# Value rows of one block gathered alternately with the next block's input rows, in two places

## The chip, the cores and the metric

One Trainium2 chip, one core of it. TensorE (PE) multiplies matrices, VectorE (DVE) and ScalarE (ACT) work elementwise, GpSimd (POOL) here only issues the indirect row gathers, SyncE (SP) issues most other transfers. All transfers share the core's 16 DMA engines. The metric is device time of the whole program in microseconds, the median over runs.

## The reference, cut to what matters

One decoder layer over 512 prompt tokens and 8 sample tokens with a cache of 4096 positions each. The part around the change is the product-key expert layer, run over blocks of 128 tokens, and beside it the sample tokens' attention over the paged cache.

```python
def one_block(xb):                       # 128 tokens
    q = jnp.einsum('td,de->te', xb, w_peer_q).reshape(PEER_BLOCK, PEER_HEADS, 2, PEER_DKEY // 2)
    s = jnp.einsum('thpc,hpkc->thpk', q, peer_sub_keys, preferred_element_type=jnp.float32)
    top_s, top_i = lax.top_k(s, PEER_TOPK)
    ...
    expert = jnp.take_along_axis(cand_i, best_pos, axis=-1)
    gate = jax.nn.softmax(best_s, axis=-1)
    u = peer_u[expert]
    act = jax.nn.gelu(jnp.einsum('thkd,td->thk', u, xb, preferred_element_type=jnp.float32), approximate=False)
    return jnp.einsum('thk,thkd->td', (gate * act).astype(peer_v.dtype), peer_v[expert])
```

## The kernel before

After projections and prompt attention the expert layer runs over four blocks of 128 tokens. For each block TensorE *routes* (`route(b)`: transposes of the normed rows, four query projections, their transposes, four products with the sub-keys; ScalarE copies each result in `route_copies(b)`), and VectorE chooses 16 experts for each of 8 heads (`top_subkeys_of`, `top_experts`; semaphore `top_done`). Then two phases follow.

In the *input phase* (u) GpSimd gathers 128 times one row of `peer_u` per token (slot k of every token, 128 rows of 4 KB in one gather), and VectorE takes the dot product with the token's row (`u_dots`, L1365). At the end ScalarE applies gelu, and TensorE and VectorE lay the weights out (`turn_w`, `W_done`). In the *value phase* (v) GpSimd gathers per token k its 128 rows of `peer_v`, with the transposed index `idxT`, and TensorE multiplies them by the token's weights (`v_phase`, L1902, two halves; the second half of row k is issued after the first half of row k + 1, and with it the row is given free). Both phases use one ring of eight slots (`RING = 8`); gather number r waits until slot r - 8 is free. In the program GpSimd's order is: inputs of block 0, values of block 0, inputs of block 1, and so on; with block 3's values the sample tokens' own rows alternate, by a list (`LAST_ROWS`).

Beside it runs the sample tokens' attention over the cache, in units: SyncE loads unit n (four pages, buffers for four units, `load_unit`), TensorE forms scores and key norms (`score_step`, L1964 to L1994), ScalarE squares (`score_units`, L879), VectorE combines eight units to a chunk (`combine_chunk`, L1396). The first 17 units (`K_U1`) stand on TensorE between route(3) and block 1's values, 15 (`K_V1`) are stepped beside block 1's value rows, one unit per eight rows from row 8 on, 28 (`K_U2`) stand between block 1's and block 2's values, and four beside block 2's values. ScalarE's gelu of a block stands behind the squares of the units before it. The constants for this part are loaded by SyncE once the last routing score of block 3 is copied, and the units' loads stand behind them.

VectorE's small work inside an input phase hangs on the dot before which it stands: the dict handed to `u_phase` gives the slot k for each piece (addition of the previous block's result `add_y`, copy of the transposed index `copy_idxT`, `finish_gates`, the queries for the cache part, chunks).

TensorE's order around the change: route(1), weights of block 0, all values of block 0, route(2), index of block 1, route(3), the cache part's queries, `K_U1`, weights of block 1, values of block 1 with `K_V1`, index of block 2, `K_U2`, block 2.

## Time and profile before

| | us |
|---|---|
| median of 3 runs | 2368.76 |
| lowest and highest | 2368.74, 2373.32 |
| span of the profiled execution | 2358.0 |
| median less profiled span | 10.8 |

| engine | busy us (share) |
|---|---|
| TensorE matmul | 1745.8 (74%) |
| VectorE | 1134.5 (48%) |
| ScalarE | 355.3 (15%) |
| GpSimd | 1232.7 (52%) |
| DMA: 784.77 MB | 333 GB/s mean |

The busy shares are averages over a program whose stages differ. Stage windows, which give each engine's busy time, the share of the DMA engines that is busy and the bytes per second between two times, tell more: their columns are start:end, length, then the busy time of TensorE's matmuls, its weight loads, VectorE, ScalarE and GpSimd. The input gathers' queue and the value gathers' queue are one (GpSimd's software queue, 547.43 MB), the cache units come through SyncE's (231.08 MB).

### The profile page before, as it was taken

To read this page: it belongs to the slowest core of one execution; us is meant where nothing else is said; L and a number is where in the kernel's file an instruction comes from. 1 tells how busy PE (TensorE), PEld (TensorE's weight loads), DVE (VectorE), ACT (ScalarE), POOL (GpSimd) and SP (SyncE) were. 2 spreads that over 40 slices of the span, in tenths; PEclk is the share of its full clock that TensorE was granted. 3 is DMA by queue.
4 is the path that set the end of the run, shared out by engine and by line. 5 is a ranking of instruction groups with operands and counts; after the bars stand their busy time and mean duration, and the time that the engine had idled before them with its cause. 6 is when DMAs were issued, how large, how long until landed. Compare 5 with 4: busy or idle time off the path is not lost.

```text
span 2358.0 us, 32033 instructions
## 1 busy us (share of the span) xinstructions
PE 1745.8 (74%) x11231; PEld 710.9 (30%) x11231; DVE 1134.5 (48%) x2727; ACT 355.3 (15%) x761; POOL 1232.7 (52%) x1076
## 2 busy tenths in 40 slices
PE   8999849857777858789998888897566223337878
PEld 2555836522011433333333333331112000011212
DVE  1543888877503666645005676691000455551361
ACT  1222223301000113221112223221000000000000
POOL 0000236657767658836567886756333444564665
PEclk9999969979999879889999799999888555558999
DMA  5104548899999899999999999999999999999988
GB/s 219 27 23 181 194 148 278 293 412 330 345 369 358 307 318 399 399 323 377 399 400 366 368 399 397 398 386 366 403 401 401 408 404 404 404 384 355 349 308 316
DMA packets 258555, 784.77 MB, mean 333 GB/s; under 512 B 36593, under 2 KB 45450, under 8 KB 254938
## 3 DMA queue, kind: packets, MB, share of 16 engines
q0 software_dynamic: 150784, 547.43, 61.3%
q1 hardware_dynamic: 106442, 231.08, 26.4%
q10 hardware_dynamic: 1168, 4.23, 0.5%
q8 instruction: 88, 1.44, 0.2%
q14 instruction: 73, 0.60, 0.1%
HBM read 775.80 MB, written 6.81 MB: 332 GB/s over the span
## 4 chain that ended last, share of the span: by engine, by line
PE 40%; DMA 29%; SPq 9%; issue 7%; DVE 7%; POOL 5%; another core or an unknown queue 2%; ACT 1%; ACTq 0%; DVEq 0%; POOLq 0%
DMA arena<-peer_v,idxT 12%; DMA arena<-peer_u,eidx 10%; PE ps L1902 9%; PE ps L1964 7%; PE ps L1588 7%; POOL arena L552 5%; DMA arena<-vn_pool 4%; SPq L514 3%; DVE arena L1365 3%; SPq L511 3%; PE ps L1828 3%; DMA arena<-kpe_pool 2%; SPq L509 2%; PE ps L1950 2%; PE ps L1703 2%
## 5 line engine op out<-in xcount | busy, mean ns | idle before, releaser
L552 POOL DMA_INDIRECT arena<-peer_u,eidx x512 | 659.2, 1287 | 666.8 <-PE ps L1817 275.2
L1365 DVE CUSTOM_DVE_ANT_0 arena<-arena 128x1024 f32<-128x1024 f32 x512 | 619.6, 1224 | 697.3 <-DMA arena<-peer_u,eidx 672.8
L552 POOL DMA_INDIRECT arena<-peer_v,idxT x512 | 519.7, 1015 | 423.9 <-PE ps L1902 309.3
L1902 PE MATMUL ps<-arena 128*32 128x512 f32 x2048 | 554.5, 646 | 115.9 <-DMA arena<-peer_v,idxT 96.7
L1964 PE MATMUL ps<-arena 128*128 128x512 f32 x512 | 314.4, 700 | 45.7 <-DMA arena<-kpe_pool 43.3
L2034 PE MATMUL ps<-arena 128*32 128x512 f32 x512 | 104.6, 882 | 265.6 <-DMA arena<-vn_pool 264.1
L1902 PEld LDWEIGHTS ps<-arena 128*32 128x32 f32 x2048 | 105.1, 114 | 448.6 <-DMA arena<-peer_v,idxT 309.4
L879 ACT ACTIVATE arena<-ps 128x512 f32<-128x512 f32 x256 | 150.8, 596 | 462.1 <-PE ps L1964 273.9
L1588 PE MATMUL ps<-arena 128*128 128x512 f32 (+3 forms) x400 | 172.0, 584 | 0.4 <-DVE arena L1028 0.4
L1950 PE MATMUL ps<-arena 128*32 128x128 f32 x2048 | 148.2, 288 | 16.4 <-issue 8.7
L1964 PEld LDWEIGHTS ps<-arena 128*128 128x128 f32 x512 | 82.8, 202 | 106.6 <-issue 56.8
L1950 PEld LDWEIGHTS ps<-arena 128*32 128x32 f32 x2048 | 73.0, 111 | 123.9 <-issue 105.3
L2034 PEld LDWEIGHTS ps<-arena 128*32 128x32 f32 x512 | 13.5, 128 | 295.9 <-DMA arena<-vn_pool 146.1
L1828 PE MATMUL ps<-arena 128*128 128x512 f32 x192 | 90.5, 630 | 7.8 <-issue 5.1
L1588 PEld LDWEIGHTS ps<-arena 128*128 128x128 f32 (+1 forms) x400 | 66.7, 171 | 92.7 <-issue 92.2
L1980 PE MATMUL ps<-arena 128*32 128x128 f32 x2048 | 88.5, 289 | 5.1 <-issue 5.1
L1980 PEld LDWEIGHTS ps<-arena 128*32 128x32 f32 x2048 | 66.7, 115 | 60.1 <-issue 50.0
L901 ACT ACTIVATE arena<-ps 128x128 f32<-128x128 f32 x32 | 8.9, 278 | 458.5 <-PE ps L2012 338.1
L1703 PE MATMUL ps<-arena 128*128 128x512 f32 x128 | 62.2, 628 | 12.5 <-DVE arena L1156 12.5
L1666 PE MATMUL ps<-con,arena 128*128 128x128 f32 x160 | 28.6, 303 | 42.5 <-ACT arena L716 39.9
L1828 PEld LDWEIGHTS ps<-arena 128*128 128x128 f32 x192 | 38.1, 202 | 54.4 <-issue 51.0
L716 ACT ACTIVATE arena<-ps,nmx 128x128 f32<-128x128 f32 (+3 forms) x64 | 33.4, 527 | 132.4 <-DVE nmx L1126 117.7
(310 smaller groups left out, 1566.8 us busy)
## 6 DMA issues: line engine op xcount, KB each, us to landing
arena<-kt_pool SPq DMA_DIRECT2D x256, 320.0 KB
arena<-vn_pool SPq DMA_DIRECT2D x256, 320.0 KB
arena<-w_q SPq DMA_DIRECT2D x16, 1024.0 KB, 13.7
arena<-w_in SPq DMA_DIRECT2D x8, 1236.0 KB, 15.7
arena<-w_o SPq DMA_DIRECT2D x16, 512.0 KB, 5.1
arena<-w_q SPq DMA_DIRECT2D x4, 2048.0 KB, 11.3
arena<-peer_u,eidx POOLq DMA_INDIRECT x512
arena<-peer_v,idxT POOLq DMA_INDIRECT x512
```

What stands on the lines that cost most here:

```text
L511: sp.dma_start(kbuf[:, slot, j, :], src[bass.ds(pg, 1), :, :] .rearrange("a p n -> p (a n)")).then_inc(k_in[slot], 16)
L552: pool.indirect_dma_start(ring[:, q % RING, :], None, table, bass.IndirectOffsetOnAxis(ap=index, axis=0)).then_inc(g[q % RING], 16)
L879: nc.scalar.activation(sqd[:, m % 2, :], ps[:, 2 + m % 2, :], ACT.Square).then_inc(sqd_done, 1)
L1365: V_.tensor_tensor_reduce(rows, rows, x, 1.0, 0.0, ALU.mult, ALU.add, acc[:, k:k + 1]).then_inc(u_used, 1)
L1588: ins = T_.matmul(ps[0:n, i, 0:w], xn[t % 2][:, c, 0:n], win[:, c, 512 * i:512 * i + w], start=(c == 0), stop=(c == DC - 1))
L1703: last = T_.matmul(ps[:, OPB[b] + i, :], mixT[b][:, c, :], wo_ch[c][:, 512 * i:512 * i + 512], start=(c == 0), stop=(c == DC - 1))
L1828: last = T_.matmul(ps[:, RB[b][i], :], xT2[:, c * P:(c + 1) * P], wq[:, c, 512 * i:512 * i + 512], start=(c == 0), stop=(c == DC - 1))
L1902: return T_.matmul(ps[32 * j:32 * j + 32, i, :], W32[:, j, c, :], ring[:, q % RING, 512 * i:512 * i + 512], start=(c == 0), stop=(c == 31) ...
L1950: last = T_.matmul(ps[32 * j:32 * j + 32, 4 + s % 2, 2 * P:3 * P], dcon[:, E_HM + 32 * (4 * par + q):E_HM + 32 * (4 * par + q) + 32], sqd[ ...
L1964: T_.matmul(ps[:, 2 + m % 2, :], wkd[:, q * P:(q + 1) * P], kbuf[:, slot, :, 512:640], start=True, stop=True).then_inc(n_ps, 1)
L1980: T_.matmul(ps[32 * j:32 * j + 32, 4 + s % 2, 0:P], qz[:, c, 2 * j + par, :], kbuf[:, slot, j, c * P:(c + 1) * P], start=(par == 0 and c = ...
L2034: T_.matmul(ps[32 * j:32 * j + 32, 4 + par, :], pTd[:, s % 2, 32 * j:32 * j + 32], kbuf[:, slot, j, 0:512], start=False, stop=True, tile_p ...
```

## The change

The rows' order becomes one list for the whole program, `SEQ`: the inputs of block 0, then for each block its first `LEAD[b]` value rows, then input rows of the next block alternating with the rest of the value rows, then the rest of the inputs. `LEAD = [72, 80, 128]`: block 0's values alternate from token 72 with block 1's inputs, block 1's from token 80 with block 2's inputs, block 2's not at all. GpSimd walks the list. TensorE's routes of blocks 2 and 3 are cut into ten steps each and stand between the value rows of block 0, at tokens 70, 73, 76 and so on up to 124. VectorE's small pieces in the input phases of blocks 1 and 2 move to later slots, since those that need the end of the previous block's values can't stand before slot 56 and 48. ScalarE stores the first result after both routes' copies.

```diff
+LEAD = [72, 80, 128]
...
-        LAST_ROWS = []
+        SEQ = [("u", 0, k) for k in range(P)]
+        for b in range(NB - 1):
+            SEQ += [("v", b, k) for k in range(LEAD[b])]
+            for k in range(P):
+                SEQ.append(("u", b + 1, k))
+                if LEAD[b] + k < P:
+                    SEQ.append(("v", b, LEAD[b] + k))
...
+            for r, (kind, b, k) in enumerate(SEQ):
+                index_ready(kind, b, k)
+                if kind == "v" and b == 1 and k % 8 == 4:
+                    gather_logf(k // 8)
+                if kind == "u" and b == 2 and k % 2 == 0 and k < NPG:
+                    gather_logf((NPG + k) // 2)
                 slot_free(r - RING)
-                if kind == "token":
-                    gather(peer_v, idxT[:, gcol(k):gcol(k) + 1], row_of(kind, k))
...
+                if kind == "u":
+                    gather(peer_u, eidx[:, k:k + 1], r)
+                elif kind == "v":
+                    gather(peer_v, idxT[:, gcol(k):gcol(k) + 1], r)
...
             route_copies(2)
+            route_copies(3)
             store_y(0)
-            route_copies(3)
...
-            u_phase(1, {8: [lambda: add_y(0)], 30: [lambda: copy_idxT(1)], 38: [lambda: finish_gates(1)],
-                        54: [decode_queries_1], 60: [decode_queries_2], 66: [log_gate_rows]})
+            u_phase(1, {64: [lambda: add_y(0)], 68: [lambda: copy_idxT(1)], 72: [lambda: finish_gates(1)],
+                        76: [decode_queries_1], 82: [decode_queries_2], 88: [log_gate_rows]})
...
-            u_phase(2, {4: [lambda: decays(0)], 6: [lambda: combine_chunk(3)], 8: [lambda: add_y(1)],
-                        16: [lambda: copy_idxT(2)], 32: [lambda: finish_gates(2)], 46: [lambda: combine_chunk(4)],
-                        56: [lambda: decays(1), total_decay], 78: [lambda: combine_chunk(5)],
+            u_phase(2, {52: [lambda: add_y(1)], 54: [lambda: copy_idxT(2)], 56: [lambda: combine_chunk(3)],
+                        60: [lambda: finish_gates(2)], 62: [lambda: decays(0)], 68: [lambda: combine_chunk(4)],
+                        74: [lambda: decays(1), total_decay], 78: [lambda: combine_chunk(5)],
                         112: [lambda: combine_chunk(6)]})
...
-            route(1)
+            for f in route_steps(1):
+                f()
             turn_w(0)
-            v_phase(0)
-            route(2)
+            steps = route_steps(2) + route_steps(3)
+            v_phase(0, {70 + 3 * i - i // 5: f for i, f in enumerate(steps)})
             turn_idx(1)
-            route(3)
```

GpSimd's instructions from the inputs of block 0 to the first values of block 1, before (`peer_u` are input gathers, `peer_v` value gathers, `logf_pool` the cache's log gates; x128 means 128 in a row):

```order
L552 DMA arena<-peer_u,eidx 128x1024 x128
L552 DMA arena<-peer_v,idxT 128x1024 x128
L552 DMA arena<-peer_u,eidx 128x1024 x128
L552 DMA arena<-peer_v,idxT 128x1024 x4
L563 DMA arena<-logf_pool,arena 128x128
```

The same stretch after, with the beginning of the alternation:

```order
L557 DMA arena<-peer_u,eidx 128x1024 x128
L557 DMA arena<-peer_v,idxT 128x1024 x72
L557 DMA arena<-peer_u,eidx 128x1024
L557 DMA arena<-peer_v,idxT 128x1024
L557 DMA arena<-peer_u,eidx 128x1024
L557 DMA arena<-peer_v,idxT 128x1024
```

After 56 such pairs 72 input gathers of block 1 follow in a row, where 128 did; in block 2 it is 48 pairs and then 80.

TensorE from the end of route(1) to route(2), before (L1902: value rows, two instructions each; L1575 transposes of the normed rows; L1828 query projections; L1835 and L1844 query transposes and scores; L1893 the weights' transpose):

```order
L1893 MATMUL ps<-con,acc 128x128
L1902 MATMUL ps<-arena 32x512 x256
L1575 MATMUL ps<-con,arena 128x128 x8
L1828 MATMUL ps<-arena 128x512 x16
L1835 MATMUL ps<-con,arena 128x128 x4
L1828 MATMUL ps<-arena 128x512 x8
```

And after (the lines are ten lower in number, L1892 being the value rows):

```order
L1883 MATMUL ps<-con,acc 128x128
L1892 MATMUL ps<-arena 32x512 x140
L1565 MATMUL ps<-con,arena 128x128 x8
L1892 MATMUL ps<-arena 32x512 x6
L1818 MATMUL ps<-arena 128x512 x8
L1892 MATMUL ps<-arena 32x512 x6
L1818 MATMUL ps<-arena 128x512 x8
L1892 MATMUL ps<-arena 32x512 x6
L1825 MATMUL ps<-con,arena 128x128 x4
```

The routes of blocks 2 and 3, which stood behind all 128 value rows, now stand in pieces between them, three rows apart.

## Rows read from the trace of the kernel before

**Rows 1.** windows: busy us (count) per engine, granted clock, DMA share, GB/s
```profile
549.00:659.00 110.00, 77.37 (x309) 15.23 (x307) 62.26 (x219) 6.55 (x10) 75.52 (x73) 0.94 0.95 351
659.00:738.40 79.40, 58.00 (x222) 8.04 (x224) 0.00 (x0) 0.00 (x0) 52.63 (x56) 1.00 0.98 365
738.40:869.00 130.60, 87.63 (x348) 46.73 (x345) 85.27 (x184) 15.97 (x30) 78.29 (x67) 0.80 0.87 311
869.00:1029.00 160.00, 134.92 (x1497) 55.84 (x1496) 84.46 (x140) 48.19 (x83) 111.94 (x71) 0.91 1.02 390
1029.00:1162.00 133.00, 123.28 (x1019) 45.76 (x1023) 66.27 (x230) 23.37 (x41) 83.55 (x82) 0.97 0.98 366
1162.00:1258.00 96.00, 93.66 (x819) 35.32 (x817) 0.48 (x1) 16.46 (x29) 58.76 (x64) 1.00 1.03 399
1258.00:1532.00 274.00, 231.27 (x2450) 94.88 (x2449) 183.08 (x293) 76.83 (x135) 208.77 (x142) 0.90 1.01 385
```

**Rows 2.** VectorE in order of time: start, length, line, operation [idle before <-releaser]
```profile
620.85 0.23 DVE L1278 CAST eidx<-eidf 128x128 uint32<-128x128 f32 x1
...
800.10 0.29 DVE L1300 CAST idxT<-ps 128x128 uint32<-128x128 f32 x1 [12.77 <-PE ps L1886]
...
850.82 0.95 DVE L1309 TENSOR_TENSOR arena<-arena 8x768 f32<-8x768 f32 x1 [16.32 <-DMA arena<-page_rows]
...
1028.63 0.29 DVE L1374 TENSOR_TENSOR acc<-acc,gate 128x128 f32<-128x128 f32 x1 [27.77 <-ACT acc L854]
...
1427.55 0.43 DVE L1396 TENSOR_SCALAR arena<-arena 128x512 f32<-128x512 f32 x1 [8.26 <-ACT arena L893]
```

**Rows 3.** two shorter windows, then TensorE's query projections from 744 to 841 us
```profile
744.00:841.00 97.00, 77.75 (x245) 41.13 (x242) 67.59 (x114) 14.97 (x27) 65.64 (x58) 0.88 0.88 322
770.00:790.00 20.00, 13.56 (x44) 6.61 (x42) 16.68 (x28) 0.60 (x1) 15.12 (x17) 0.91 1.03 412
...
L1828 PE MATMUL ps<-arena 128*128 128x512 f32 x128 | 59.9, 626 | 6.3 <-issue 5.1 <-ACT arena L800 1.2
```

**Rows 4.** one window, input gathers alone; then GpSimd in order of time
```profile
869.00:1029.00 160.00, 98.45 (x62) 0.91 1.02 390
...
659.06 0.94 POOL L552 DMA_INDIRECT arena<-peer_v,idxT  x1 [0.49 <-PE ps L1902]
...
986.38 1.54 POOL L552 DMA_INDIRECT arena<-peer_u,eidx  x1 [0.31 <-issue]
...
1161.51 0.94 POOL L552 DMA_INDIRECT arena<-peer_v,idxT  x1 [0.93 <-PE ps L1902]
...
1243.76 0.94 POOL L552 DMA_INDIRECT arena<-peer_v,idxT  x1 [0.30 <-issue]
```

**Rows 5.** TensorE in order of time: last matmuls (L1994) of single cache units
```profile
875.98 0.42 PE L1994 MATMUL ps<-arena 32*32 32x128 f32 x8
...
883.07 0.42 PE L1994 MATMUL ps<-arena 32*32 32x128 f32 x8
...
952.46 0.42 PE L1994 MATMUL ps<-arena 32*32 32x128 f32 x8
...
983.74 0.42 PE L1994 MATMUL ps<-arena 32*32 32x128 f32 x8
...
1026.20 0.42 PE L1994 MATMUL ps<-arena 32*32 32x128 f32 x8
...
1531.76 0.42 PE L1994 MATMUL ps<-arena 32*32 32x128 f32 x8
```

**Rows 6.** groups of GpSimd: busy us, mean ns | idle before <-releasers
```profile
L552 POOL DMA_INDIRECT arena<-peer_u,eidx x512 | 659.2, 1287 | 666.8 <-PE ps L1817 275.2 <-DVE acc L1365 260.6 <-issue 112.4
L552 POOL DMA_INDIRECT arena<-peer_v,idxT x512 | 519.7, 1015 | 423.9 <-PE ps L1902 309.3 <-issue 100.1 <-DVE acc L1365 7.5
```

**Rows 7.** transfers by source: issuing queue, number, KB of each
```profile
arena<-kt_pool SPq DMA_DIRECT2D x256, 320.0 KB
...
arena<-kpe_pool SPq DMA_DIRECT2D x256, 16.0 KB
```

More of the change, by code:

```diff
@@ L384, in gcol, with row_of @@
             return 32 * (i % 4) + i // 4
-        LAST_ROWS = []
+        SEQ = [("u", 0, k) for k in range(P)]
[5 more added lines that the diff above has]
+                    SEQ.append(("v", b, LEAD[b] + k))
         for k in range(P):
             if S_U <= k < S_U + BD:
-                LAST_ROWS.append(("u", k - S_U))
+                SEQ.append(("su", SBLK, k - S_U))
             if S_V <= k < S_V + BD:
-                LAST_ROWS.append(("v", k - S_V))
-            LAST_ROWS.append(("token", k))
-        def row_of(kind, k):
-            return 2 * P * (NB - 1) + P + LAST_ROWS.index((kind, k))
-        def v_row(b, k):
-            return 2 * P * b + P + k if b < NB - 1 else row_of("token", k)
+                SEQ.append(("sv", SBLK, k - S_V))
+            SEQ.append(("v", NB - 1, k))
+        PLACE = {row: r for r, row in enumerate(SEQ)}
+        def row_of(kind, b, k):
+            return PLACE[kind, b, k]
         @block.sync
@@ L565, in gather_logf, with index_ready @@
                                         ).then_inc(lg_gathered, 16)
-            for b in range(NB):
-                if b:
-                    pool.wait_ge(top_done, b + 1)
-                for k in range(SLOTS):
-                    if b == 0 and k % 32 == 0:
+            def index_ready(kind, b, k):
+                if kind == "u" and b == 0:
+                    if k % 32 == 0:
                         if k < 96:
```

71 lines of the change are left out of this document (22 added, 49 removed).

## The prediction

> **What bounds the kernel now.** I read the stage windows first [rows 1]: from 549 us on the DMA engines are busy 0.95 to 1.03 of nearly every stage, so what counts is how many bytes per microsecond a stage moves. With row gathers and the cache stream together the rate is 399 GB/s (1162 to 1258 us); value gathers alone make 365; the stage from 738 to 869 us makes only 311. Then I read who was late there. VectorE waits 12.77 us for the transposed index of block 1, then 16.32 us for the decode constants, and after the last dot 27.77 us for ScalarE's gelu, which stands behind the cache units' squares [rows 2]. The index and the constants come late because TensorE routes blocks 2 and 3 only after all value rows of block 0: 77.75 us of work in a 97 us stretch [rows 3]. VectorE meanwhile had block 1's experts at 621 us [rows 2] and is idle in the whole stage from 659 to 738. The last look is at the pace of cache units [rows 5]: two in a row end 7.09 us apart when the data is there, but three take 31.3 us (10.4 each) while gathers compete, and 28 units of block 2 end at 1532.2.
>
> Sizes: one gather is 128 rows of 4 KB, 0.524 MB; a cache unit is 4 x (320 + 16) KB, 1.376 MB [rows 7]. Nothing is added or taken away in bytes, matmuls or dots. The change is worth only what it does to idle DMA time, and the most that stands to be won is small: at 399 GB/s, the stages from 549 to 1029 us lose 13, 7, 29 and 4 us (length x (1 - rate/399)), 53 in all; from 1029 to 1532 they lose 11, 0 and 10.
>
> **First place: value rows 72 to 127 of block 0 with input rows 0 to 55 of block 1.** Value row 72 is issued at 659.1 [rows 4]. From there 112 gathers alternate. The nearest row for their pace is that of value gathers alone, 56 in 79.4 us, 1.42 us each [rows 1]; the other end is 399 GB/s, 1.31 each. I take 1.42, since no cache units run beside them: 159 us, to 818. TensorE has to do in it 56 value rows (58.0 us, the same window) and the routes of blocks 2 and 3 (77.75 us), 136 us, so it is not the bound on average; the steps lie at every third token. VectorE has 56 dots of 1.23 us, far less. The two waits of 12.77 and 16.32 us go: the transposed index is made right after value row 127 and wanted at input 68, the constants are asked for when the last score is copied (token 124) and wanted at input 76. The waiting instructions now are the y-addition at 64, the index copy at 68 and the gates at 72; what is behind them on VectorE are dots, but each waits for something that TensorE and ScalarE finished before or at 818, so I cost them at nothing. On ScalarE the y store moves behind both routes' copies, so that it no longer blocks the copies; nothing waits for that store before the next block's h load.
>
> What is late next is the start of the cache units, which now hangs on input 82 instead of 60. Between 818 and that row the DMA carries 27 gathers (14.2 MB), four prefetched units (5.5) and the constants (1.3), 21.0 MB at 390 GB/s (the stage 869 to 1029): 54 us, plus some 5 us of VectorE's small copies for the queries. Start: 877, where before it is 876.4 - 7.1 = 869.3. So here 8 us are lost. But fewer input rows are left to compete: 45 instead of 67, at 1.89 us each (62 in the stage from 869, the last issued at 986.4 [rows 4]) 85 us. Before, ten units took 83.6 us from the start (the tenth ends at 952.9). Seven remain, between 7.1 and 10.6 us each (the last four before took 42.5 us); I take 8: 56 us. The 17 units end at 877 + 141 = 1018, before at 1026.6. **First place: -9 us.** If the mixing runs at 1.31 us it is 12 us better; if every one of the eight query-projection steps (59.9/8 = 7.5 us each [rows 3]) holds back the ring by what exceeds three gathers, 4 us, it is 32 us worse.
>
> **Second place: value rows 80 to 127 of block 1 with input rows 0 to 47 of block 2.** I count from the end of the 17 units, T (1026.6 before). Value row 80 is issued at T + 135 [rows 4], unchanged. The block's experts are chosen by then: VectorE is idle from 1162 to 1258 before. Then 96 gathers and six cache units, 50.3 + 8.3 = 58.6 MB at 399 GB/s: 147 us; TensorE needs 48 x 1.04 + 6 x 7.09 = 92. Last value row T + 282 (before T + 217), and TensorE is through 14 us later, as before: T + 296. Now 28 cache units stand against 80 input rows, where it was 128. Their floor is TensorE's, 28 x 7.09 = 198.5, and the DMA's, 80.5 MB at 399, 202. VectorE does not dot past input 68 before chunk 4 is there (unit 39) nor past 78 before chunk 5 (unit 47); the same wait shows already with 128 rows, 8.26 us [rows 2]. While it waits the gathers stand still and the units have the DMA: 16 x 7.09 = 113 us. Then 12 units against 50 rows (94 us): ten in 84 us as at the start of the first run, two at 7.1: 98. Sum 211, with a copy 212. End T + 508, before T + 505.6. **Second place: +2 us**, between -8 (the floor of 202) and +32 (below).
>
> Behind it (block 2's values, block 3) nothing is moved: it starts with four units and eight rows prefetched as now, at the DMA's limit.
>
> **Sum.** 2358.0 - 9 + 2 = 2351.0 for the span; the median of the runs lies 10.8 us above the profiled span, so **2361.8 us**, 0.3% faster. What a measurement of this kernel can tell from no change is about 0.2%, 4.7 us.
>
> **Rivals.**
>
> (a) *The units are never starved.* If the two streams shared the DMA evenly, a unit would come every 1.376/0.2 = 6.9 us and TensorE's 7.09 would hold. First run bounded by 45 rows, 17 units and eight value rows, 51.2 MB at 399: 128 instead of 141. Tail 202 instead of 212. With the mixing at 1.31, another 12. Together -35: 2327. For it: two units with their data there do end 7.09 us apart; against: the 10.4 us per unit [rows 5]. The Trainium skill (DMA: Bandwidth & Descriptors, "Queues, rings and completion order") says that each DMA engine takes turns between queues packet by packet; with equal packets that would be this rival. The trace has the cache stream at 1.376/10.4 = 132 GB/s of about 399, a third, so equal shares are not what it shows.
>
> (b) *The tail of cache units takes over as the bound; slower.* Place: 28 units after value row 127 of block 1. If the 80 rows compete all the time (151 us) instead of standing at 68 and 78, ten units take 84, then 67/10.4 = 6.4, and 11.6 remain at 8: 244 instead of 212, +32; half of the pauses, +25. It decides from a tail above 214 us (where second place eats the first's gain it is 219). 2387. For it: the units' count is unchanged while the rows beside them fall from 128 to 80, so the DMA runs half used in the end, and in the first run 27.77 us of exactly this are seen.
>
> (c) *The gather engine gets slow beside dots.* An input gather takes GpSimd 1287 ns, a value gather 1015 [rows 6], 0.30 us between two. If all alternating gathers go at 1.59 us, 112 x 0.17 = 19 us and 96 x 0.06 = 6 us: 2387. Against: 412 GB/s, 1.27 us per gather, is seen with VectorE 83% busy with dots [rows 3], so most of the 1287 is back pressure. The Trainium skill (SBUF — State Buffer, "Who interferes with whom") has a VectorE instruction with two SBUF inputs contending with a GpSimd instruction that reads SBUF; the dots are of that form, and it speaks against this change. The 412 GB/s stretch shows that it need not set the pace.
>
> (d) *The ring stops at the route steps.* All eight rows of the ring are issued in order, so a value row that waits 7.5 us behind a projection holds input rows back too: +32 at most: 2394. Against: eight rows are 11.4 us of DMA work, longer than the step.
>
> **Chances.** Forecast 0.40, (a) 0.25, (b) 0.15, (c) 0.08, (d) 0.12. The forecast's own spread (the 7.1 to 10.6 for seven units alone is 25 us wide) puts 0.22 of its 0.40 below -0.2%, 0.13 within, 0.05 above. Faster 0.22 + 0.25 = 0.47; within 0.2% 0.13 + 0.05 from weak forms of (b) to (d) = 0.18; slower 0.35. Range 2333 to 2394: its own range alone would be 2348 to 2376.
>
> **What would show it.** Input row 0 of block 1 is gathered near 660 and value row 127 near 818 (at 840 or more (c) or (d) is at work, at 806 (a)). No VectorE wait of over 5 us at inputs 68 and 76 of block 1. First cache unit begins near 877, the 17th ends near 1018. Between the value rows' end and the 28th unit of block 2 lie about 212 us, with VectorE waits at inputs 68 and 78 of some tens of microseconds; under (b) the waits are short and the tail is over 235. From the first value row of block 2 on, both traces run alike; if they do not, the sum is wrong, whatever the two places do.

## The result, and the profile after

The change makes the kernel slower: 2440.86 us (median of 4 runs, 2433.61 to 2461.23) against 2371.04 on the same chip, a ratio of 1.0315 with the interval [1.0273, 1.0357]. Two later comparisons on other chips gave 1.0259 [1.0195, 1.0323] and 1.0385 [1.0323, 1.0447]. The page of the kernel after, its span, busy times and DMA rate:

```profile
span 2442.4 us, 31673 instructions
PE 1779.6 (73%) x11231; PEld 721.6 (30%) x11231; DVE 1134.8 (46%) x2727; ACT 356.6 (15%) x761; POOL 1192.3 (49%) x1076
DMA packets 258553, 784.76 MB, mean 321 GB/s; under 512 B 36593, under 2 KB 45450, under 8 KB 254938
```

Bytes, dots and matmuls are the same as before, and VectorE and ScalarE are as long busy (TensorE is 34 us longer busy, GpSimd 40 us less). The mean rate fell from 333 to 321 GB/s. So the question is in which stages DMA time was lost. Stage windows of the kernel after (columns as in [rows 1]), from the first value row of block 0 to the end of the 60th cache unit:

```profile
556.00:671.00 115.00, 82.35 (x320) 16.49 (x319) 62.49 (x221) 6.66 (x10) 73.94 (x74) 0.91 0.93 340
671.00:845.00 174.00, 141.92 (x462) 49.72 (x459) 66.13 (x107) 15.90 (x27) 118.35 (x110) 0.94 0.91 330
845.00:915.00 70.00, 12.57 (x103) 6.57 (x103) 49.03 (x124) 0.94 (x3) 42.57 (x35) 0.57 0.96 365
915.00:983.00 68.00, 59.88 (x609) 24.79 (x607) 47.33 (x81) 17.87 (x31) 55.79 (x41) 0.90 1.00 379
983.00:1061.00 78.00, 72.95 (x867) 31.22 (x870) 7.40 (x12) 27.67 (x49) 12.51 (x9) 0.96 0.85 282
1061.00:1198.00 137.00, 124.87 (x1070) 48.15 (x1070) 66.53 (x231) 26.10 (x44) 83.86 (x84) 0.99 0.98 368
1198.00:1370.00 172.00, 113.84 (x735) 34.69 (x728) 56.25 (x91) 15.37 (x27) 122.48 (x115) 0.82 0.96 347
1370.00:1384.00 14.00, 12.31 (x99) 4.91 (x95) 6.70 (x12) 2.24 (x4) 8.83 (x9) 0.89 0.93 323
1384.00:1456.00 72.00, 65.34 (x688) 26.64 (x692) 30.64 (x48) 22.26 (x41) 29.57 (x21) 0.88 0.92 330
1456.00:1517.00 61.00, 58.59 (x730) 25.21 (x720) 20.50 (x30) 22.56 (x40) 16.64 (x10) 1.00 0.85 272
1517.00:1613.00 96.00, 89.01 (x1008) 37.24 (x1012) 67.68 (x112) 31.23 (x55) 73.78 (x47) 0.93 0.99 373
```

Take for each row its length times (1 - rate/399), as the prediction did. Before [rows 1], the stages lose 52 us up to the end of the 17 units and 21 from there to the end of the 60th, 73 in all. After, the first five rows lose 17 + 30 + 6 + 3 + 23 = 79 and the other six 11 + 22 + 3 + 12 + 19 + 6 = 73, together 152. The stretch is 1057 us long where it was 983. So 79 us more of DMA time are lost, and the stretch is 74 us longer.

Counted along the time axis, the profiled span grew by 84.4 us:

| stretch | before | after | difference |
|---|---|---|---|
| up to value row 72 of block 0 (nothing changed there) | 659 | 671 | +12 |
| from there to the end of unit 17 (first place) | 368 | 390 | +22 |
| to value row 80 of block 1 | 135 | 137 | +2 |
| to the end of unit 60 (second place) | 370 | 415 | +45 |
| to the end | 826 | 829 | +3 |

The first +12 lies ahead of everything the change touches. The same stretch was 664 us in another run of the kernel before (e9) and 661 in one of the kernel after (e10), so single executions scatter by as much. What the change costs is about 70 us by the medians, a third of it in the first place and two thirds in the second.

Now who was late. TensorE and VectorE of the kernel after in order of time: start, length, line, operation [idle before <-releaser]. L1917 is the first instruction of the cache part's queries, L1364 the gate products behind the last dot, L1386 the first instruction of a chunk:

```profile
901.44 1.02 PE L1917 MATMUL ps<-con,arena 8*128 8x8 f32 x8 [46.50 <-DVE arena L1315]
...
1063.31 0.29 DVE L1364 TENSOR_TENSOR acc<-acc,gate 128x128 f32<-128x128 f32 x1 [68.64 <-ACT acc L844]
...
1456.61 0.43 DVE L1386 TENSOR_SCALAR arena<-arena 128x512 f32<-128x512 f32 x1 [39.27 <-ACT arena L883]
...
1516.92 0.43 DVE L1386 TENSOR_SCALAR arena<-arena 128x512 f32<-128x512 f32 x1 [39.62 <-ACT arena L883]
```

The waits of [rows 2] for the transposed index (12.77) and the constants (16.32) are gone, as forecast. In their place TensorE stands 46.50 us for the queries, because VectorE makes them only at inputs 76 and 82, and VectorE then stands 68.64 us for gelu behind the 17 units, where it was 27.77. In this wait the ring is full, GpSimd issues 9 gathers in 78 us, and the rate falls to 282 GB/s. In block 2 the two chunk waits of nearly 40 us each do the same (21 and 10 gathers in 72 and 61 us, 330 and 272 GB/s), where the one of [rows 2] was 8.26.

The two alternations themselves are slow as well. GpSimd's groups, busy us, mean ns | idle before <-releasers: first the kernel before in its value rows 659 to 738.

```profile
L552 POOL DMA_INDIRECT arena<-peer_v,idxT x56 | 52.6, 940 | 27.2 <-PE ps L1902 17.6 <-issue 9.6
```

Then the kernel after, 671 to 845 (first two lines) and 1198 to 1370:

```profile
L557 POOL DMA_INDIRECT arena<-peer_v,idxT x55 | 59.6, 1084 | 39.2 <-PE ps L1892 27.1 <-issue 12.1
L557 POOL DMA_INDIRECT arena<-peer_u,eidx x55 | 58.9, 1070 | 16.8 <-issue 16.5 <-PE ps L1892 0.3
...
L557 POOL DMA_INDIRECT arena<-peer_v,idxT x47 | 51.3, 1091 | 28.8 <-PE ps L1892 11.7 <-issue 10.1 <-remote 7.1
L557 POOL DMA_INDIRECT arena<-peer_u,eidx x47 | 49.0, 1042 | 15.3 <-issue 13.7 <-PE ps L1892 1.6
L568 POOL DMA_INDIRECT arena<-logf_pool,arena x21 | 22.6, 1075 | 6.4 <-issue 6.4
```

In the first, 147 of 174 us are GpSimd's own (59.6 + 58.9 busy, 12.1 + 16.5 between two instructions), and 27.4 are waits for value rows that TensorE has not yet used. In the second, 153 of 172 us are its own, 29 of them (22.6 + 6.4) for 21 gathers of log gates, small in bytes but as long as any other on this engine. So GpSimd's own instructions and the gaps between them fill 85 to 89% of both, which the prediction did not reckon with.

Part of that own time is VectorE's doing. GpSimd and VectorE of the kernel after in order of time, two gathers and the two dots beside them:

```profile
701.49 1.23 DVE L1355 CUSTOM_DVE_ANT_0 arena<-arena 128x1024 f32<-128x1024 f32 x1 [1.31 <-DMA arena<-peer_u,eidx]
701.77 1.76 POOL L557 DMA_INDIRECT arena<-peer_u,eidx  x1 [0.30 <-issue]
703.84 0.94 POOL L557 DMA_INDIRECT arena<-peer_v,idxT  x1 [0.30 <-PE ps L1892]
704.14 1.23 DVE L1355 CUSTOM_DVE_ANT_0 arena<-arena 128x1024 f32<-128x1024 f32 x1 [1.41 <-DMA arena<-peer_u,eidx]
```

The first gather starts while a dot is running and ends 0.81 us after the dot does; the second starts ahead of its dot and takes 0.94 us. In the first alternation 38 of 109 recorded gathers start with more than 0.13 us of a dot left and take 1.34 us on average, and the other 71 take 0.93 to 0.95; in the second it is 31 of 93, at 1.33 us. Together that is 15 us of GpSimd's time in each alternation.

### The profile page after: what moved, and what is told of

Read it like the earlier page. It is cut to its first block, busy times and chain, and to the rows that moved or that the text cites. A ratio compares the mean times of both kernels' runs of the same rounds, so it can differ in the third digit from the quotient of the medians.

```text
span 2442.4 us, 31673 instructions
## 1 busy us (share of the span) xinstructions
PE 1779.6 (73%) x11231; PEld 721.6 (30%) x11231; DVE 1134.8 (46%) x2727; ACT 356.6 (15%) x761; POOL 1192.3 (49%) x1076
## 4 chain that ended last, share of the span: by engine, by line
PE 44%; DMA 29%; POOL 9%; DVE 7%; issue 6%; SPq 3%; ACT 1%; another core or an unknown queue 1%; DVEq 0%; ACTq 0%; POOLq 0%
DMA arena<-peer_v,idxT 12%; DMA arena<-peer_u,eidx 12%; PE ps L1954 9%; PE ps L1892 9%; POOL arena L557 8%; PE ps L1578 7%; DMA arena<-vn_pool 4%; PE ps L1818 4%; PE ps L1940 3%; DVE arena L1355 3%; PE ps L1970 2%; PE ps L1693 2%; SPq L516 2%; DMA arena<-kpe_pool 2%; SPq L514 1%
## 5 line engine op out<-in xcount | busy, mean ns | idle before, releaser
L557 POOL DMA_INDIRECT arena<-peer_u,eidx x512 | 612.9, 1197 | 732.2 <-DVE acc L1355 326.5
L557 POOL DMA_INDIRECT arena<-peer_v,idxT x512 | 530.5, 1036 | 484.4 <-PE ps L1892 347.1
L1892 PE MATMUL ps<-arena 128*32 128x512 f32 x2048 | 576.3, 658 | 183.2 <-DMA arena<-peer_v,idxT 152.7
L1954 PE MATMUL ps<-arena 128*128 128x512 f32 x512 | 311.6, 694 | 11.2 <-DMA arena<-kpe_pool 7.8
L2024 PE MATMUL ps<-arena 128*32 128x512 f32 x512 | 105.8, 893 | 271.2 <-DMA arena<-vn_pool 261.5
L1892 PEld LDWEIGHTS ps<-arena 128*32 128x32 f32 x2048 | 108.0, 115 | 520.1 <-DMA arena<-peer_v,idxT 353.8
L1940 PE MATMUL ps<-arena 128*32 128x128 f32 x2048 | 150.9, 292 | 13.1 <-issue 10.3
L1954 PEld LDWEIGHTS ps<-arena 128*128 128x128 f32 x512 | 82.6, 202 | 73.7 <-issue 61.5
L1970 PE MATMUL ps<-arena 128*32 128x128 f32 x2048 | 91.0, 287 | 10.6 <-issue 10.6
L1818 PE MATMUL ps<-arena 128*128 128x512 f32 x192 | 89.1, 619 | 1.6 <-ACT arena L790 1.6
L1693 PE MATMUL ps<-arena 128*128 128x512 f32 x128 | 61.2, 620 | 12.2 <-DVE arena L1146 12.2
L1386 DVE TENSOR_SCALAR arena<-arena 128x512 f32<-128x512 f32 x8 | 3.4, 423 | 142.4 <-ACT arena L883 129.3
L1640 PE MATMUL ps<-arena 96*128 96x128 f32 (+7 forms) x128 | 55.0, 515 | 2.3 <-issue 1.4
```

The source lines that it names most:

```text
L557: pool.indirect_dma_start(ring[:, q % RING, :], None, table, bass.IndirectOffsetOnAxis(ap=index, axis=0)).then_inc(g[q % RING], 16)
L1640: T_.matmul(ps[:, bank, j * w:(j + 1) * w], QT[b][0:kd, hh, :], KT[0:kd, hh, 0:w], start=True, stop=False, skip_group_check=True)
L1693: last = T_.matmul(ps[:, OPB[b] + i, :], mixT[b][:, c, :], wo_ch[c][:, 512 * i:512 * i + 512], start=(c == 0), stop=(c == DC - 1))
L1818: last = T_.matmul(ps[:, RB[b][i], :], xT2[:, c * P:(c + 1) * P], wq[:, c, 512 * i:512 * i + 512], start=(c == 0), stop=(c == DC - 1))
L1892: return T_.matmul(ps[32 * j:32 * j + 32, i, :], W32[:, j, c, :], ring[:, q % RING, 512 * i:512 * i + 512], start=(c == 0), stop=(c == 31) ...
L1940: last = T_.matmul(ps[32 * j:32 * j + 32, 4 + s % 2, 2 * P:3 * P], dcon[:, E_HM + 32 * (4 * par + q):E_HM + 32 * (4 * par + q) + 32], sqd[ ...
```

## The experiments

Edits are against the kernel after unless said otherwise. Ratios are to the kernel before on the same chip. The runs fall on four chips: the first four on one, e5 to e8 and later e13 and e14 on one, e9 to e12 on one, e15 to e17 on one. The change itself was run beside the kernel before on the last two of them, as e10 and e17. The chip of e5 to e8 and that of e17 give the kernel before the same time (2304.16 and 2304.75 us), so e5 to e8 are read against e17 below.

**One place alone.** The other place is as in the kernel before, with its slots in `u_phase` (and for e2 its TensorE and ScalarE order).

```diff
-LEAD = [72, 80, 128]
+LEAD = [72, 128, 128]
```

> Only the first place: block 0's value rows alternate from token 72 with block 1's inputs; block 1's values and block 2's inputs as before the change. The trace of the changed kernel has the 17th cache unit end at 1061 instead of 1027 us, 7 us of it already there when the first value row of block 0 is gathered, and the 28th unit of block 2 80 us late. Theory P (both places lose, the second more): +27 us on the kernel before, about 2398, ratio 1.011. Theory Q (the second place loses only because the first hands it a bad start): the whole loss or nearly, 2425 or more. My prediction had -9 us here.

Measured: 2397.94 us, 1.0152 [1.0094, 1.0210], 28 us over the kernel before.

```diff
-LEAD = [72, 80, 128]
+LEAD = [128, 80, 128]
```

> Only the second place: block 1's value rows alternate from token 80 with block 2's inputs; block 0's values, the routes of blocks 2 and 3 and block 1's inputs as before. Theory P: +46 us, about 2417, ratio 1.019, with 96 gathers from value row 80 on taking about 170 us. Theory Q: +5 us at most. If the two places' losses add up, e1 and e2 together make the change's 70 us.

Measured: 2414.48 us, 1.0204 [1.0154, 1.0254], 45 us. The two together are 73, the change about 70: the losses add within the scatter (the sum of the two ratios' excesses is 3.6%, the change's ratios give 2.6 to 3.9), and neither place brings anything. By the medians the second is the larger; the two intervals overlap.

**The queries earlier, log gates later.** e3 moves VectorE's small pieces so that the queries come first.

```diff
-u_phase(1, {64: [add_y(0)], 68: [copy_idxT(1)], 72: [finish_gates(1)],
-            76: [decode_queries_1], 82: [decode_queries_2], 88: [log_gate_rows]})
+u_phase(1, {58: [add_y(0)], 60: [copy_idxT(1)], 62: [decode_queries_1],
+            67: [decode_queries_2], 72: [finish_gates(1)], 88: [log_gate_rows]})
```

> The change with VectorE's work for the cache queries at inputs 62 and 67 of block 1 instead of 76 and 82 (the y addition, index copy and gates move with it to 58, 60 and 72). In the changed kernel TensorE stands still for 46.5 us before these queries, until 901 us, and VectorE waits 68.6 us for the last of the 17 units after its dots. Theory R (the start of the 17 units is what the first place loses): the first unit starts some 18 to 22 us earlier and the kernel gets 18 to 22 us faster, about 2421. Rival S (the first place loses by the pace of alternating gathers and DMA bytes, and the units only compete earlier): under 6 us, 2435 or more.

Measured: 2411.89 us, 1.0185 [1.0128, 1.0242]. The same two waits as above, in e3:

```profile
880.03 1.02 PE L1917 MATMUL ps<-con,arena 8*128 8x8 f32 x8 [16.65 <-DVE arena L1315]
...
1044.17 0.29 DVE L1364 TENSOR_TENSOR acc<-acc,gate 128x128 f32<-128x128 f32 x1 [37.23 <-ACT acc L844]
```

TensorE's wait fell from 46.50 to 16.65 and VectorE's from 68.64 to 37.23. The median is 32 us below e4 on the same chip, which is like the change up to block 2. The late queries thus cost some 30 us, and this belongs only to where pieces were put.

e4 takes 16 of the log-gate gathers out of the second alternation.

```diff
-if kind == "u" and b == 2 and k % 2 == 0 and k < NPG:
-    gather_logf((NPG + k) // 2)
+if kind == "u" and b == 2 and 48 <= k < 48 + NPG // 2:
+    gather_logf(NPG // 2 + k - 48)
```

> The change with the second half of the log-gate gathers (16 small ones on the same GpSimd queue) issued beside input rows 48 to 63 of block 2, behind the alternation, instead of beside rows 0 to 30 inside it. In the changed kernel the 96 alternating gathers of the second place take 172 us, and GpSimd issues 21 log-gate gathers between them, at 1.25 us each at least. Theory G (GpSimd's issue sets the pace there): the alternation gets 16 x 1.3 = 21 us shorter, and as 28 units follow it unchanged the kernel 15 to 21 us faster, about 2422. Rival H (the ring in order sets it: a value row is freed only after the next value row has landed, two gathers later): under 5 us.

Measured: 2443.66 us, 1.0319 [1.0261, 1.0377], no gain that can be seen against the change's three ratios. Windows of e4, the alternation and what comes after it:

```profile
1188.00:1346.00 158.00, 109.36 (x736) 34.56 (x731) 56.33 (x91) 15.27 (x27) 111.64 (x100) 0.84 1.00 376
1346.00:1396.00 50.00, 29.66 (x144) 10.21 (x141) 31.69 (x49) 5.52 (x10) 39.51 (x35) 0.64 0.77 250
```

The alternation fell from 172 to 158 us (it is 173 in e2 and e3 on this chip), so those gathers did hold it up. But from its end to the end of unit 33 it took 47 us instead of 20. TensorE in order of time there:

```profile
1360.83 0.30 PE L1970 MATMUL ps<-arena 128*32 128x128 f32 x2 [0.46 <-issue]
1362.26 0.27 PE L1970 MATMUL ps<-arena 128*32 128x128 f32 x1 [1.13 <-issue]
```

From 1357 to 1392 us it runs most of its small matmuls singly or by twos, some 0.7 us apart, and waits for nothing that the profile shows. What holds it there I could not find out.

**Re-sharing the units.** Both edits put more units beside block 1's value rows, one step per row from token 80 on; e5 takes them from the tail (17, 21 and 22 units instead of 17, 15 and 28), e6 from the first run (11, 21 and 28, with chunk 2 at input 24 of block 2).

```diff
-K_U1, K_V1, K_U2, K_V2 = range(0, 17), range(17, 32), range(32, 60), range(60, 64)
+K_U1, K_V1, K_U2, K_V2 = range(0, 17), range(17, 38), range(38, 60), range(60, 64)
...
-v_phase(1, {}, lambda k: step_beside(K_V1, 8, k))
+v_phase(1, {}, dense_steps)
```

> The change with six cache units taken out of the run of 28 behind block 1's values and stepped beside its alternating value rows: from token 80 on one unit per four rows instead of per eight, 21 units beside the values, 22 behind. In the changed kernel the alternation takes 172 us with TensorE busy 114 of them, and the 28 units behind it take 229 us, 8.0 each after the first, near TensorE's own 7.1, while the DMA engines move 272 to 330 GB/s for 133 us. Theory U (the second place loses because the units stand behind a stream that has lost 48 of its 128 gathers; gathers moved forward shorten nothing there): tail 6 x 8 = 48 us shorter, alternation up to 15 us longer: 33 to 48 us faster, about 2400. Rival V (the loss is the slow alternation itself): the units' TensorE work in it delays the ring further and the gain is under 15 us.

> The change with the same denser stepping beside block 1's values, but the six units taken out of the first run of 17, which becomes 11; the run of 28 stays. (Chunk 2 is combined at input 24 of block 2 then, since its last unit comes in the alternation.) In the changed kernel VectorE waits 68.6 us for the last of the 17 units, and the DMA engines move 282 GB/s from 983 to 1061 us. Theory U: 6 x 7.1 = 43 us earlier start of block 1's values, alternation up to 15 us longer: 28 to 43 us faster, about 2405. Rival V: under 15 us.

Measured: e5 2362.34 us, 1.0243 [1.0209, 1.0277]; e6 2356.39 us, 1.0237 [1.0200, 1.0274]. Windows of e5, second alternation and tail:

```profile
1174.00:1344.00 170.00, 133.85 (x1224) 47.06 (x1215) 55.58 (x90) 31.01 (x54) 124.68 (x115) 0.97 1.03 395
1344.00:1538.00 194.00, 176.03 (x2041) 74.04 (x2039) 125.95 (x200) 63.08 (x110) 129.45 (x86) 0.95 1.00 381
```

With six units more in it the alternation takes 170 us, at 395 GB/s, where it is 165 in e17, and the tail shrank from 227 to 194 us. So most of the six units' bytes went in DMA time that the alternation of the change leaves unused. Against e17 the gain is 32 us in e5 and 38 in e6, near what theory U had expected (33 to 48 and 28 to 43); the ratios of both lie below all three of the change.

**What slows the alternation.** e7 issues both halves of a value row at once in the alternating rows, so that its slot is free one row earlier. e8 puts all route steps behind value row 127.

```diff
 late = k
+if b < NB - 1 and k >= LEAD[b]:
+    half(k, 1).then_inc(v_used, 1)
+    late = None
```

> The change with the second half of a value row multiplied right behind its first half while rows alternate, instead of behind the next value row's first half. So the slot is free two gathers earlier. Theory H (the ring in order sets the alternation's pace, 1.55 and 1.79 us per gather where I took 1.42 and 1.53): GpSimd's waits for TensorE, 27 us in the first alternation and 13 in the second, fall, both alternations get 8 to 13 us shorter, the kernel 10 to 25 us faster. Rival G (GpSimd's issue and the DMA set it): under 5 us, 2436 or more.

```diff
-v_phase(0, {70 + 3 * i - i // 5: f for i, f in enumerate(steps)})
-turn_idx(1)
+v_phase(0)
+turn_idx(1)
+for f in steps:
+    f()
```

> The change with the routes of blocks 2 and 3 behind block 0's value rows again (rows still alternate). Theory D (the route steps between the rows hold the ring back): the first alternation falls from 174 us to 112 x 1.42 = 159 or below; but the routes, 78 us of TensorE, now stand before the cache part's queries, so the first unit starts at about 845 - 15 + 90 = 920 plus the constants and queries, 20 us: 25 us later than in the changed kernel, and the kernel is 10 to 25 us slower than it. Rival: the alternation stays at 174 us, and the kernel is 35 to 45 us slower.

Measured: e7 2383.53 us, 1.0343 [1.0309, 1.0376]; its first alternation took 169 us where e17's took 180, its second 164 where e17's took 165 (those of e5 and e6 are longer because they hold more units). The median is 11 us below e17's, but the two ratios' intervals overlap, so a gain is likely and not shown. e8 2409.53 us, 1.0448 [1.0418, 1.0478]. Windows of e8, its first alternation and what follows; then GpSimd's groups in that alternation:

```profile
652.00:808.00 156.00, 96.84 (x231) 10.14 (x228) 66.66 (x108) 0.00 (x0) 116.21 (x111) 0.62 0.98 372
808.00:915.00 107.00, 81.17 (x339) 42.65 (x339) 45.12 (x107) 15.98 (x30) 40.41 (x33) 0.85 0.60 212
```

```profile
L557 POOL DMA_INDIRECT arena<-peer_v,idxT x56 | 63.7, 1137 | 23.3 <-PE ps L1892 14.0 <-issue 9.3
L557 POOL DMA_INDIRECT arena<-peer_u,eidx x55 | 53.4, 971 | 16.8 <-issue 16.8
```

Without route steps in it the alternation takes 156 us, 1.39 per gather, where it takes 177 to 180 with them (e5, e6, e17), 21 to 24 us more. GpSimd's waits for value rows are 14.0 us, half of the 27.4 in the kernel after, and its own part (143 us) is nearly as there. Behind it the routes now run with little beside them, 212 GB/s for 107 us: the constants are asked for after the last route, and VectorE of e8 stands for them with the ring full:

```profile
898.18 0.95 DVE L1299 TENSOR_TENSOR arena<-arena 8x768 f32<-8x768 f32 x1 [54.10 <-DMA arena<-page_rows]
```

**Controls, and all pieces shared anew.** e9 is the kernel before, e10 the change, again. e11 has 11, 27 and 22 units, three units per eight rows from token 80, chunk 2 at input 24 and the queries of e3; e12 adds e4 and e7 to it.

```diff
-K_U1, K_V1, K_U2, K_V2 = range(0, 17), range(17, 32), range(32, 60), range(60, 64)
+K_U1, K_V1, K_U2, K_V2 = range(0, 11), range(11, 38), range(38, 60), range(60, 64)
```

> The kernel before, once more and beside the next three, for its trace on the same chip: the chip of the runs e5 to e8 gave it 2304 us, that of e1 to e4 2370. All theories: ratio 1.00.

> The changed kernel once more, for its trace and its ratio beside the kernel before on this chip. All theories: ratio 1.03, as at first. If it is far from 1.03, the ratios of e5 to e8 have to be read against this one.

> The change with its units shared out anew and the queries early: 11 cache units before block 1's values instead of 17, 27 beside them (one per eight rows up to token 80, then three per eight), 22 behind instead of 28, and VectorE's query work at inputs 62 and 67 of block 1. Theory U + R (the change loses because TensorE's cache units stand alone where gathers were taken away, and start late): the single gains were 29 us (queries early), 17 and 18 us (six units out of the tail, six out of the first run); with most of the sum left, 50 us: ratio 1.008 to 1.012. Rival W (an alternating row costs more whatever stands beside it, 15 to 25 us in each place): the units crowd the alternation, and the ratio stays at 1.015 or more. Under 1.00 the alternation itself would be a gain that only the shares hid.

> e11 with, in addition, the second half of the log-gate gathers behind the alternation and no deferral of the second half of an alternating value row. Theory: both shorten the alternations (14 us in e4's trace; 6 to 7 us each in e7's beside e5's and e6's), which counts once no run of units swallows it: 10 to 20 us below e11. Rival (the DMA's bytes set the pace once the units are spread): under 5 us below e11.

Measured: e9 2356.02 us, 0.9993 [0.9958, 1.0028]; e10 2429.48 us, 1.0259 [1.0195, 1.0323]; e11 2361.65 us, 1.0014 [0.9976, 1.0052]; e12 2376.18 us, 1.0060 [1.0031, 1.0089]. Windows of e11, from the first alternation to the end of the tail:

```profile
662.00:841.00 179.00, 148.11 (x464) 51.19 (x464) 66.34 (x107) 15.91 (x27) 115.56 (x112) 0.91 0.89 323
841.00:888.00 47.00, 19.12 (x171) 9.16 (x171) 35.29 (x103) 2.20 (x6) 33.12 (x24) 0.64 1.03 390
888.00:1002.00 114.00, 84.78 (x905) 34.76 (x907) 73.06 (x122) 30.87 (x52) 92.38 (x60) 0.83 1.03 399
1002.00:1136.00 134.00, 127.14 (x1040) 46.47 (x1039) 57.15 (x216) 22.65 (x40) 85.64 (x84) 0.98 1.01 382
1136.00:1327.00 191.00, 174.66 (x1699) 69.43 (x1694) 59.97 (x97) 45.90 (x81) 126.17 (x115) 1.00 1.02 385
1327.00:1529.00 202.00, 182.28 (x2073) 75.98 (x2068) 127.65 (x203) 63.84 (x112) 119.74 (x87) 0.95 1.01 379
```

The whole loss is gone (e11 is 68 us below e10 on the same chip): with the units shared anew and the queries early, the stages from the end of the first alternation on run at 379 to 399 GB/s, and unit 60 ends at 1529 us, in the trace of e9 at 1539. The alternations are no shorter for it (179 and 192 us, in e10 175 and 174), so a long alternation is no loss as long as enough bytes go through it. But nothing is won either. e12, with the two pieces that were to shorten the alternations, is slower than e11 by 15 us, against what I expected: its first alternation is 9 us shorter, its second 7 longer, and from there to unit 60 it takes 217 us instead of 202. In the first 50 us of that stretch the rate is 301 GB/s, where e11 has 398, and single matmuls 0.7 us apart stand there as in e4.

**Is there anything in the alternation itself?** e13 alternates only from token 100 in the first place, second place as before; e14 is the first place alone with early queries, 13, 15 and 32 units and later chunks; e15 has no alternation, only the route steps between the value rows of block 0. e16 and e17 are the kernel before and the change on e15's chip. In e13 to e15 VectorE's pieces stand as early as each order lets them, the queries at inputs 34 and 39 in e13, 62 and 67 in e14, 14 and 20 in e15. The edit of e15's order:

```diff
-LEAD = [72, 80, 128]
+LEAD = [128, 128, 128]
```

> Only the first place, and from token 100: 28 pairs instead of 56, so that the cache queries can stand at inputs 34 and 39 of block 1 and 89 input rows are left beside the 17 units; block 2 as in the kernel before. Theory U + R (what counts is that the units start early and have gathers beside them): the first unit starts near 850 instead of 873 us, the 17 take as long as before, and the kernel is 10 to 25 us faster than the kernel before, ratio 0.990 to 0.996. Theory W (alternation with route steps costs over 20 us by itself): the start is not earlier and the ratio 1.000 to 1.010.

> Only the first place, from token 72 as in the change, with the queries at inputs 62 and 67, 13 cache units before block 1's values, 15 beside them and 32 behind, beside block 2's 128 input rows; chunks 3 to 6 are combined at later inputs there. e1 gave +28 us for the place as it was changed, the early queries took 29 off the whole change, and four units fewer before block 1's values are worth 4 x 7.1 = 28, given back in part (4 units x 3.5 us of DMA = 14) in block 2. Theory U + R: -10 us, ratio 0.993 to 0.998. Theory W: 1.005 or more.

> No alternation at all: only the route steps of blocks 2 and 3 stand between block 0's value rows 70 to 124, and the queries at inputs 14 and 20 of block 1; everything behind as in the kernel before. It parts what moving the routes does from what alternating does. Theory X (the route steps between value rows are the loss in the first place): value rows 72 to 127 take 77 + 55 to 78 us, the units start that much less 50 us earlier than before, near 850, and the kernel is within 10 us of the short alternation's ratio of 1.008. Theory W (the alternation is): the ratio is 1.00 or under, and the alternation adds what e13 has above it.

> The kernel before for its trace beside e15 (and e5 to e8, e13, e14, if the chip is the same one, which gives it 2303 us). Ratio 1.00.

> The change for its trace and ratio on this chip. Ratio 1.026 to 1.034.

Measured: e13 2322.56 us, 1.0076 [1.0049, 1.0103]; e14 2334.97 us, 1.0134 [1.0091, 1.0176]; e15 2331.11 us, 1.0108 [1.0051, 1.0164]; e16 2302.46 us, 0.9986 [0.9960, 1.0012]; e17 2394.58 us, 1.0385 [1.0323, 1.0447]. In e13 the first unit ends at 846 us, as in e16, no earlier, and the kernel is 20 us slower than the kernel before; e14 is 32 us slower in spite of its early queries. Both had been expected to be faster, so starting the units early and sharing them anew does not rescue the first place by itself. e15 has no alternating row and is 26 us slower all the same, about as much as e1 (28 by its median, 22 to 50 by its interval): the route steps between value rows alone cost what the first place loses, and no run shows that alternating adds to it there.

Windows of e15 from value row 72 of block 0 to the first value rows of block 1:

```profile
652.00:764.00 112.00, 111.33 (x453) 44.29 (x452) 0.00 (x0) 15.30 (x26) 51.32 (x55) 1.00 0.74 263
764.00:827.00 63.00, 21.33 (x206) 11.29 (x201) 43.93 (x114) 3.92 (x8) 45.36 (x31) 0.65 1.01 381
827.00:976.00 149.00, 125.07 (x1404) 52.26 (x1408) 91.38 (x152) 43.53 (x76) 98.76 (x79) 0.92 1.02 393
976.00:1029.00 53.00, 4.92 (x31) 1.31 (x28) 38.80 (x65) 3.11 (x4) 29.27 (x30) 0.53 1.03 398
```

And the same of e16, the kernel before on this chip:

```profile
652.00:723.00 71.00, 57.72 (x220) 7.86 (x220) 0.00 (x0) 0.00 (x0) 51.47 (x55) 1.00 1.02 403
723.00:846.00 123.00, 91.85 (x421) 47.08 (x419) 90.85 (x193) 17.76 (x33) 92.19 (x73) 0.85 0.98 364
846.00:996.00 150.00, 126.52 (x1425) 53.13 (x1424) 78.04 (x129) 44.36 (x78) 104.65 (x67) 0.91 1.02 391
```

In e15 TensorE fills the 112 us (111.33 busy) and the value rows come 41 us later. The units start 19 us and end 20 us earlier than in e16. Then TensorE does 4.92 us of work in 53, because the inputs come in until 1014 us, at 398 GB/s: block 1's ninth value row is at 1029 us, where e16 has it at 1001. That is the point of the first place. From the last value row of block 0 on, the stretch is a matter of bytes, and what the routes leave unused there is only 123 x (1 - 364/399) = 11 us on this chip (on the other [rows 1] 29). Moving them out can win no more than that, and in e15 the value rows with route steps between them leave 38 us of DMA time unused (112 us at 263 GB/s).

The stages of the runs that are to be held against e17, from the first gather's start to the last one's, in us:

| run | first alternation | second alternation | from there to the end of unit 60 | median |
|---|---|---|---|---|
| e17, the change | 180 | 165 | 227 | 2394.58 |
| e5, units from the tail | 177 | 170 | 194 | 2362.34 |
| e6, units from the first run | 179 | 172 | 232 | 2356.39 |
| e7, no deferral | 169 | 164 | 231 | 2383.53 |
| e8, routes behind | 156 | 166 | 233 | 2409.53 |

So neither place for the routes is good: with them behind the value rows the first alternation is 24 us shorter, but the kernel 15 us slower, since the constants and the queries come later.

## Why the prediction was wrong, step by step

The forecast of 2361.8 us had the sign wrong; the value measured lies 47 us above the range. Of the 91 us between the forecast span of 2351.0 and 2442.4, 12 stand ahead of the change and 3 behind it. The prediction's last term, 10.8 us from profile to median, was that of one execution: after the change the median lies 1.5 us below the profiled span. The rest, by the prediction's own steps:

| step | forecast | measured |
|---|---|---|
| first alternation | 159 | 174 |
| last value row to the start of the units | 59 | 70 |
| 17 units | 141 | 146 |
| to value row 80 of block 1 | 135 | 137 |
| second alternation | 147 | 172 |
| its end to the start of the tail | 14 | 14 |
| tail of 28 units | 212 | 229 |

- **What bounds the kernel** was read rightly, the DMA rate, and so was the small size of what can be won. That nothing behind unit 60 changes is right too (826 and 829 us).
- **The pace of the alternation** is the step that failed most, 15 + 25 us. I took it from the DMA: 1.42 us per gather, and 399 GB/s for the second. But the engine that issues was near its own limit: at [rows 4] a gather takes 0.94 us and 0.30 follow. In an alternation its own part is 1.3 us per instruction, and log gates count as whole gathers: the second has 96 + 21 = 117 of them, 145 us at the very best and 153 as measured, where I had 147 from bytes alone; e4, with 16 of them taken out, had it 14 us shorter. In the first come the holds by value rows that stand behind route steps, rival (d), which e8 puts at 21 to 24 us; I had priced it rightly (at most 32) and given it 0.12. That eight rows are 11.4 us of DMA work, which I held against it, did not prevent them. What such a stage costs is the cache units' bytes that could have gone beside it (e5, e11), not its length.
- **The start of the units.** The sum had 27 gathers and 21.0 MB up to input 82, and it came 11 us later than that. The cost was there in the plan, since I saw that the start hung on input 82; what I did not ask is what the late start does to VectorE. It waited 68.64 us instead of 27.77, and e3 got about 30 us back by placing four pieces earlier.
- **The tail.** The 212 us rested on gathers that stand still while the units have the DMA. They did (39.27 and 39.62 us), but TensorE is busy 65.34 of 72 and 58.59 of 61 us there, and the DMA ran at 330 and 272 GB/s. The term that was too small is 16 units at 7.09 us, 113: they took 72 + 61 = 133, 8.3 each, and the 12 after them 96 where I had 98. Rival (b) had named the tail as the place, and the 229 are half of its extra, but not by its mechanism: it had short waits and rows that compete all the time.
- **Rival (a)** is refuted, and the reason is in the packets. DMA of the kernel before from 1335 to 1385 us, queue, packets, MB and share (q0 carries the gathers, q1 the cache units):

```profile
q0 software_dynamic: 3657, 13.29, 67.0%
q1 hardware_dynamic: 3651, 6.54, 35.7%
```

The packets are equal in number, and the cache's are half as large (1.79 KB against 3.63). A unit's 1.376 MB are 768 such packets, which then go with 768 of gathers, 2.79 MB: 4.17 MB at 399 GB/s are 10.4 us, the pace of [rows 5]. The Trainium skill (DMA: Bandwidth & Descriptors, "Queues, rings and completion order") states that engines take turns between queues packet by packet; what it calls a packet holds several descriptors, so the profile's equal counts agree with it if both queues' packets hold as many, which no view here shows. The prediction held the third of the bytes against the rival; what speaks against it is the unequal packet size.

- **Rival (c)** was at work, and my argument against it was wrong. A gather takes 0.94 us with VectorE idle and 1.04 to 1.09 on average in the alternations, some 15 us in each. I put the 1287 ns of the input gathers down to back pressure from the DMA. But over the whole trace of the kernel before, 96% of the recorded gathers take, to within 0.05 us, 0.94 us or 0.81 more than what is left of the dot that runs when they start, whichever is more, and of the 71 in the first alternation of the kernel after that start with at most 0.13 us of a dot left none is longer than 0.95. So it is the dots. In the 412 GB/s stretch a dot had only 0.14 to 0.27 us left whenever a gather started beside one, and so the gathers took 0.95 to 1.08 us. The Trainium skill (SBUF — State Buffer, "Who interferes with whom") would have it so beside dots with two SBUF inputs, and the trace agrees. No run took the dots away, so what the 15 us are worth in the kernel's time stays open.
- **The range** ended at 2394 because (b), (c) and (d) were taken as alternatives. They can all be at work at once, and here something of each was (17 us of the tail, 15 of GpSimd's time in each place, 21 to 24 by route steps). Their three prices together, 25 + 25 + 32, would have put its end at 2444.

Left open: the stretch of single matmuls in e4 (which may also be why e12 gained nothing), whether e7 gains, and how the 45 us of the second place divide between its alternation and its tail. No version was faster than the kernel before; e11 equals it.

## What to carry to other kernels

Where the DMA is the bound, moving work together can win only the DMA time that the stages leave unused; count that first (length times one less the rate over the best rate), and then look whether the engine that issues the transfers can go faster at all: its instructions times their length plus the gap between them, small transfers counted as full ones. When a row stream is brought forward, whatever was hidden beside it has to be shared out anew, and each small piece that another engine waits for must stand as early as its data allow, for a late one stops the ring and with it the bytes. Where two rivals' mechanisms can be at work at once, add their prices for the end of the range.

## What the runs showed of the hardware

- The same kernel takes 2302 to 2305 us on two chips and 2356 to 2371 on the others. Of the 58 us between the traces of e9 and e16, 34 lie between the first value row and the first cache unit, where value gathers and routes run. The kernel before on a slower chip (e9), from value row 72 of block 0, to be held against e16 above:

```profile
664.00:741.00 77.00, 57.06 (x216) 8.25 (x216) 0.00 (x0) 0.00 (x0) 51.56 (x55) 0.98 0.98 368
741.00:873.00 132.00, 87.78 (x352) 46.62 (x351) 86.94 (x186) 16.08 (x30) 82.68 (x68) 0.80 0.89 317
880.00:1030.00 150.00, 125.12 (x1398) 52.23 (x1396) 76.76 (x125) 43.07 (x75) 102.89 (x67) 0.92 1.02 388
```

  368 and 317 GB/s stand against 403 and 364, while the stretch of the 17 units is 150 us on both. Only ratios on one chip can be compared, or times on chips that give the kernel before the same time.
- An indirect gather of 128 rows takes GpSimd 0.94 us, and 0.30 us pass before the next. If one of VectorE's dots is running when it starts, it ends 0.81 us after the dot. A dot that starts after the gather does not lengthen it.
- TensorE can fall into stretches, 35 us long in e4, in which small matmuls come singly 0.7 us apart behind no wait that is seen. The granted clock of e4 was 0.85 from 1356 to 1366 us, when this had begun, and 0.50, the lower of its two levels, from 1366 to 1396.
